# A chunked recurrent scan: growth factors in a tile of their own, operands and state updates at other levels of the inverse

## The chip, the cores and the metric

One core of a Trainium2 chip runs the whole kernel. Its engines work beside each other and meet at semaphores: TensorE (PE in the profile, with PEld for its weight loads), VectorE (DVE), ScalarE (ACT), GpSimd (POOL), and SyncE (SP), which issues most DMAs. Each engine takes its own instructions strictly in order. The metric is the device time in microseconds (us), the median of several executions.

## The reference, cut to what matters

Two layers of a diffusion backbone over 256 latent and 256 context tokens. One of the three branches of a layer is a bidirectional RWKV-7 time mixing: in each of 8 heads a 64 x 64 state is carried over the tokens, forwards and backwards.

```python
def wkv_scan(r, w, k, v, a, b, S0, reverse):
    def step(S, inp):
        rt, wt, kt, vt, at, bt = inp
        sa = jnp.einsum('bhvk,bhk->bhv', S, at)
        S = S * wt[:, :, None, :] + sa[..., None] * bt[:, :, None, :] + vt[..., None] * kt[:, :, None, :]
        return S, jnp.einsum('bhvk,bhk->bhv', S, rt)
    S_fin, ys = lax.scan(step, S0, xs, reverse=reverse)
...
y_ctx, s_ctx = rwkv_mix(pr_c, zero_state, *rw)
y_lat, _ = rwkv_mix(pr_l, s_ctx, *rw)
```

The context's final state is the start of the latent tokens' scan. In the last layer the context's outputs are not needed, only its state. Everything else (Fourier mixing, latent attention, merge, a mixture of 16 experts) is outside the change.

## The kernel before

The scan runs in chunks of 64 tokens: `STEPS` = 8 per layer, k = 0 to 3 over the context, k = 4 to 7 over the latent tokens. Each step treats both directions, d = 0 and 1, and all heads at once in tiles of 128 partitions x 256 columns (`RJ` = 4 pairs of heads x 64). Layer 0 reads an output from every step; in layer 1 `streams(l, k)` is true for k = 4 to 7 only.

What a step computes:

- `cumulate` (DVE, L1549/L1552) sums the log decays within the chunk into `L`. From it POOL subtracts (`decays_before`, L1899), and ACT makes three exponentials: `decays` into `Rq` (L1188), `decays_before` into `E3` (L1194) and `growths` (L1199), which overwrites `L`.
- `totals` (DVE, L1560) copies the last column of the decays, by which the state is scaled; `queries` (POOL, L1909) then overwrites `Rq`, so it waits for `totals`. It exists only where the step streams an output.
- `operands` (DVE, L1569 to L1571) multiplies keys with `E3` and with the growths, and signals `keys`. PE's `couple` makes the 64 x 64 coupling matrix from them, `begin` (DVE, L1577 to L1581) masks it, `grams` and `masks` (DVE, L1588 to L1592) give the others.
- The coupling matrix is inverted by doubling: `LEVELS` = 2, 4, 8, 16, 32 are n = 0 to 4 in the code and are called level zero to level four here. At each level POOL's `blocks` (L1892) picks the off-diagonal blocks, PE's `join` multiplies, ACT copies (L1237), PE's `grow` multiplies, DVE adds and transposes (L1600, L1602; the last level L1605).
- For the chunk before, k - 1, PE runs `correct` (needs the state), `solve`, `readout` and `update`; DVE's `read` adds the output (L1612) and `update` renews the state (L1620, L1621).

All PE products go through L715. The order in each engine's queue is written out by hand. PE, in step k: `couple(k)`, `correct(k-1)`, `grams(k,0)`, `solve(k-1)`, `grams(k,1)`, then five levels, each join 0, join 1, grow 0, grow 1, with the transposes of the next operands in level zero, a readout each in levels one and two, `update(k-1)` in level three and the next chunk's values in level four. PE's `correct` waits for the signal of DVE's L1621. POOL's order, which the change leaves as it is, in step k:

```python
for n in range(len(LEVELS)):
    for d in range(2):
        blocks(k, n, d)
    if more and n == 1:
        for d in range(2):
            decays_before(k + 1, d)
    if more and n >= 3:
        queries(k + 1, n - 3)
```

While a scan runs, no weights are loaded: its tiles lie where the weights go.

Of the kernel before, what the change touches and what calls it, by code (L numbers as in the profile page):

```python
# [9 lines left out]
ALU = mybir.AluOpType  # L10
ACT = mybir.ActivationFunctionType
# [23 lines left out]
DECAY = math.exp(-0.5)  # L35
# [54 lines left out]
def build(nc, xT, cT, vec, fng, rb, rw, w_ada, w_in, headw, w_ukv, lora, w_a, w_b, w_c, w_out,  # L90
# [4 lines left out]
    with ExitStack() as ctx:  # L95
# [5 lines left out]
        def sem(name):  # L101
            if name not in sems:
                sems[name] = ctx.enter_context(nc.semaphore(name))
            return sems[name]
# [70 lines left out]
        def piece(units, of=(0, 1, 2)):  # L175

            for n in of:
                if taken[n] + units * 256 <= spare[n].shape[1]:
                    taken[n] += units * 256
                    return spare[n][:, taken[n] - units * 256:taken[n]]  # L180
            raise AssertionError("no room")

        def quads(x, n=1):
            x = x.rearrange("p (x j n) -> p x j n", x=n, n=CH)
            return x if n > 1 else x[:, 0]
# [16 lines left out]
            ONCE[name] = [quads(piece(1)) for d in range(2)]  # L202
        ONCE["U"] = ONCE["RHS"]
        PF = [quads(piece(1)) for d in range(2)]
        PS = [[quads(raw[d][:, 256:512]) for d in range(2)]] * (len(LEVELS) - 1) + [PF]
        BTS = [ONCE[name] for name in ("BT0", "BT1", "BT0", "BT1", "MT")]

# [90 lines left out]
        STEPS = 2 * NCH  # L298

        def columns(k, d):  # L300

            s, c = k // NCH, k % NCH
            return slice((1 - s) * SEQ + (NCH - 1 - c if d else c) * CH, (1 - s) * SEQ + (NCH - 1 - c if d else c) * CH + CH)
# [17 lines left out]
        def nth(N, d, per=1, n=0):  # L321

            return 2 * per * N + per * d + n + 1

        def level(N, n, d):

            return 2 * (len(LEVELS) * N + n) + d + 1

        def halved(N, n, d):

# [703 lines left out]
        def _(act):  # L1034
# [31 lines left out]
            for l in range(DEPTH):  # L1066
# [116 lines left out]
                def decays(k, d):  # L1183

                    act.wait_ge(sem("cumulated"), nth(l * STEPS + k, d))
                    if k >= 2 and streams(l, k - 2):
                        act.wait_ge(sem("readout"), 2 * readouts(l, k - 2) - 1 + d)
                    act.activation(flat(TWICE["Rq"][k % 2][d]), flat(ONCE["L"][d]), ACT.Exp, scale=-DECAY)\  # L1188
                       .then_inc(sem("exps"), 1)

                def decays_before(k, d):
                    act.wait_ge(sem("before"), nth(l * STEPS + k, d))
                    x = flat(TWICE["E3"][k % 2][d])
                    act.activation(x, x, ACT.Exp, scale=-DECAY).then_inc(sem("exps"), 1)  # L1194

                def growths(k, d):
                    x = flat(ONCE["L"][d])
                    act.wait_ge(sem("exps"), nth(l * STEPS + k, d, 3, 1))
                    act.activation(x, x, ACT.Exp, scale=DECAY).then_inc(sem("exps"), 1)  # L1199

                def turns(k, d):
                    act.wait_ge(sem("turns"), carried(l, k, d))
# [2 lines left out]
                def values(k):  # L1205
                    for d in range(2):
                        act.wait_ge(sem("values"), nth(l * STEPS + k, d))
                        act.copy(flat(TWICE["Vt"][k % 2][d]), part(d, 1, 1)).then_inc(sem("values_held"), 1)
# [10 lines left out]

                log_decays(0)  # L1220
                for d in range(2):
                    decays(0, d)
                    decays_before(0, d)
                    growths(0, d)
                values(0)
                for k in range(STEPS):
                    more = k + 1 < STEPS
                    if k:
                        correct(k - 1)
                    if more:  # L1230
                        log_decays(k + 1)
                    if k:
                        solve(k - 1)
                    for n in range(len(LEVELS)):
                        for d in range(2):
                            act.wait_ge(sem("joined"), level(l * STEPS + k, n, d))
                            act.copy(under(PS[n][d], n, d), under(part(d, 3, 0).rearrange("p (j n) -> p j n", n=CH), n, d))\  # L1237
                               .then_inc(sem("joined_copied"), 1)
                            if n == 0 and more:
                                turns(k, d)  # L1240
                        if more and n in (1, 2):
                            decays(k + 1, n - 1)
                            decays_before(k + 1, n - 1)
                            growths(k + 1, n - 1)
                    if more:
                        values(k + 1)
                correct(STEPS - 1)
# [105 lines left out]
        def _(dve):  # L1353
# [22 lines left out]
            for l in range(DEPTH):  # L1376
# [164 lines left out]
                def cumulate(k, d):  # L1541

                    N, p = l * STEPS + k, k % 2
                    lw, L = TWICE["E3"][p][d], ONCE["L"][d]
                    dve.wait_ge(sem("decays"), nth(N, d))
                    if N:
                        dve.wait_ge(sem("keys"), nth(N - 1, d))
                    if d == 0:
                        dve.tensor_tensor_scan(flat(L), con_("reset", RJ * CH), flat(lw), 0.0,  # L1549
                                               ALU.mult, ALU.add).then_inc(sem("cumulated"), 1)  # L1550
                    else:
                        dve.tensor_tensor_scan(flat(L)[:, ::-1], con_("reset", RJ * CH), flat(lw)[:, ::-1], 0.0,  # L1552
                                               ALU.mult, ALU.add).then_inc(sem("cumulated"), 1)

                def totals(k, d):

                    N, p = l * STEPS + k, k % 2
                    end = CH - 1 if d == 0 else 0
                    dve.wait_ge(sem("exps"), nth(N, d, 3))
                    dve.tensor_copy(total[:, k % 3, d, :].unsqueeze(2), TWICE["Rq"][p][d][:, :, end:end + 1])\  # L1560
                       .then_inc(sem("totals"), 1)

                def operands(k, d):

                    N, p = l * STEPS + k, k % 2
                    dve.wait_ge(sem("exps"), nth(N, d, 3, 2))
                    if k:
                        dve.wait_ge(sem("turns"), carried(l, k - 1, d))
                    tt(TWICE["E3"][p][d], KK[:, :, columns(k, d)], TWICE["E3"][p][d], ALU.mult)  # L1569
                    tt(ONCE["bKk"][d], KDs[d][:, :, columns(k, d)], ONCE["L"][d], ALU.mult)  # L1570
                    tt(ONCE["bE2"][d], B[d][:, :, columns(k, d)], ONCE["L"][d], ALU.mult).then_inc(sem("keys"), 1)  # L1571

                def begin(k, d):

# [49 lines left out]
                for d in range(2):  # L1624
                    cumulate(0, d)
                for d in range(2):
                    totals(0, d)
                for d in range(2):
                    operands(0, d)
                for k in range(STEPS):  # L1630
                    more = k + 1 < STEPS
                    for d in range(2):
                        begin(k, d)
                    for d in range(2):
                        masks(k, d)
                        if more:
                            cumulate(k + 1, d)
                    for n in range(len(LEVELS)):
                        for d in range(2):
                            grow(k, n, d)  # L1640
                        if more and n in (2, 3):
                            totals(k + 1, n - 2)
                            operands(k + 1, n - 2)
                        if k and n in (1, 2):
                            read(k - 1, n - 1)
                        if k and n == 4:
                            for d in range(2):
                                update(k - 1, d)
                for d in range(2):
                    read(STEPS - 1, d)  # L1650
                over()
# [200 lines left out]
        def _(pool):  # L1852
# [15 lines left out]
            for l in range(DEPTH):  # L1868
# [25 lines left out]
                def decays_before(k, d):  # L1894

                    N = l * STEPS + k
                    pool.wait_ge(sem("cumulated"), nth(N, d))
                    x = TWICE["E3"][k % 2][d]
                    tt(x, ONCE["L"][d], x, ALU.subtract).then_inc(sem("before"), 1)  # L1899

                def queries(k, d):

                    if not streams(l, k):
                        return
                    N = l * STEPS + k
                    pool.wait_ge(sem("totals"), nth(N, d))
                    pool.wait_ge(sem("exps"), nth(N, d, 3))
                    x = TWICE["Rq"][k % 2][d]
                    tt(x, R[:, :, columns(k, d)], x, ALU.mult).then_inc(sem("queries"), 1)  # L1909

# [164 lines left out]
```

## Time and profile before

| | |
|---|---|
| median of 3 runs | 2402.03 us (2399.49 to 2406.5) |
| the profiled execution's own time | 2396.57 us |
| its span in the trace | 2394.8 us |
| PE busy | 2128.6 us, 89% of the span |
| DVE, ACT, POOL busy | 727.4, 490.0, 278.8 us |
| mean granted TensorE clock | 0.951 |
| scan of layer 0, from and to | 424.4 to 641.1 us |
| scan of layer 1 | 1651.8 to 1852.0 us |

All times in the trace are counted from the span's start. A matmul's end is modelled, so that a busy PE is a PE with work in flight. In a timeline row, the bracket at the end is how long the engine had been idle and what released it. The granted clock is 1.00 at 2.4 GHz and 0.50 at 1.2 GHz; a value between is a mean over the stretch.

### The profile page before, as it was taken

The numbers are of one execution on the slowest core, as the hardware profiler recorded it, in microseconds if no ns is written. First come the engines' busy times: TensorE is split into PE (matmuls) and PEld (weight loads), VectorE is DVE, ScalarE is ACT, GpSimd is POOL, SyncE is SP. The second block draws the span as 40 slices with busy tenths as digits, with TensorE's granted clock in tenths as the row PEclk, the third lists the DMA queues.
The fourth block names the chain that finished last, engine by engine and source line by source line (L and its number), as shares of the span: only waits on it lengthen the run. The fifth ranks groups of instructions, "written<-read, shape, count | busy, mean of one in ns | idle before, by whom it ended". The sixth has DMA issues, their size and how long they took to land. (4 is left out here: it accounts for less than half of the span.)

```text
span 2394.8 us, 53930 instructions
## 1 busy us (share of the span) xinstructions
PE 2128.6 (89%) x23930; PEld 1357.3 (57%) x23930; DVE 727.4 (30%) x1768; ACT 490.0 (20%) x1120; POOL 278.8 (12%) x463
## 2 busy tenths in 40 slices
PE   6999999899799999999999779998988899977784
PEld 2454444789644444446566464554888787744442
DVE  1023334777431011310100032445775311200001
ACT  2122322333130000301111132323332301100011
POOL 0000000444100001101111100001442000011111
PEclk8999999899999999999999989998999999989896
DMA  7149816000121312448999821210000345899993
GB/s 281 58 146 331 313 49 236 3 4 4 55 88 53 105 53 105 170 166 324 381 383 383 306 92 43 67 49 1 4 4 13 144 145 190 281 379 381 383 383 120
DMA packets 182915, 399.91 MB, mean 167 GB/s; under 512 B 6656, under 2 KB 29952, under 8 KB 182496
## 3 DMA queue, kind: packets, MB, share of 16 engines
q1 hardware_dynamic: 170528, 361.94, 42.0%
q0 software_dynamic: 8576, 23.08, 2.6%
q10 hardware_dynamic: 3648, 12.45, 1.8%
q8 instruction: 134, 2.20, 0.4%
q14 instruction: 29, 0.24, 0.0%
HBM read 365.47 MB, written 31.98 MB: 166 GB/s over the span
## 5 line engine op out<-in xcount | busy, mean ns | idle before, releaser
L481 PE MATMUL ps<-H,memory 128*128 128x512 f32 (+2 forms) x1728 | 616.7, 513 | 11.8 <-DMA memory<-in_w_in 10.0
L481 PEld LDWEIGHTS ps<-H,memory 128*128 128x128 f32 (+1 forms) x1728 | 328.8, 191 | 287.3 <-issue 251.3
L715 PE MATMUL ps<-memory 64*64 64x32 f32 (+2 forms) x10112 | 333.1, 230 | 42.9 <-DVE memory L1621 17.6
L978 PE MATMUL ps<-memory 128*32 128x256 f32 x5120 | 304.5, 400 | 60.2 <-DMA memory<-in_eu 58.6
L715 PEld LDWEIGHTS ps<-memory 64*64 64x64 f32 x10112 | 318.9, 143 | 53.9 <-DVE memory L1621 19.1
L481 PE MATMUL ps<-memory 128*128 128x512 f32 (+4 forms) x960 | 336.3, 500 | 8.3 <-issue 3.0
L978 PEld LDWEIGHTS ps<-memory 128*32 128x32 f32 x5120 | 192.0, 115 | 170.6 <-issue 89.8
L481 PEld LDWEIGHTS ps<-memory 128*128 128x128 f32 (+2 forms) x960 | 175.1, 185 | 159.1 <-issue 140.2
L1003 PE MATMUL ps<-memory 128*32 128x256 f32 x2560 | 144.8, 380 | 4.9 <-ACT memory L1324 3.8
L1892 POOL TENSOR_TENSOR memory<-memory,cons 128x256 f32<-128x256 f32 x160 | 120.3, 769 | 122.5 <-DVE memory L1577 93.0
L1956 POOL DMA_DIRECT2D expert_rows<-memory x128 | 69.3, 541 | 436.5 <-DVE memory L1825 412.6
L1003 PEld LDWEIGHTS ps<-memory 128*32 128x32 f32 x2560 | 80.0, 110 | 59.4 <-ACT memory L1324 10.1
L1260 ACT ACTIVATE memory<-ps 128x512 f32<-128x512 f32 (+1 forms) x48 | 23.5, 490 | 333.9 <-PE ps L481 333.9
L1693 DVE TENSOR_TENSOR memory<-memory,ps 128x512 f32<-128x512 f32 (+1 forms) x32 | 17.8, 555 | 214.8 <-PE ps L481 214.8
L1237 ACT COPY memory<-ps 128x128 f32<-128x128 f32 x160 | 42.9, 268 | 163.5 <-PE ps L715 163.3
L715 PE MATMUL ps<-cons,memory 64*64 64x64 f32 x1408 | 59.2, 231 | 12.5 <-issue 10.2
L1820 DVE TENSOR_TENSOR memory<-memory,ps 128x256 f32<-128x256 f32 x16 | 6.7, 421 | 183.9 <-ACT memory L1322 183.9
L715 PEld LDWEIGHTS ps<-cons,memory 64*64 64x64 f32 x1408 | 52.2, 145 | 14.8 <-issue 12.0
L1600 DVE TENSOR_TENSOR memory<-memory,ps 128x128 f32<-128x128 f32 x128 | 34.6, 270 | 81.5 <-PE ps L715 80.6
L1602 DVE STREAM_TRANSPOSE memory<-memory 128x256 f32<-128x256 f32 x128 | 57.0, 446 | 4.4
L1825 DVE COPY memory<-ps 128x256 f32<-128x256 f32 x32 | 13.6, 425 | 137.7 <-PE ps L1003 137.7
L1929 POOL TENSOR_TENSOR memory<-H 128x512 f32<-128x512 f32 (+1 forms) x2 | 2.0, 995 | 442.0 <-ACT H L1270 442.0
(251 smaller groups left out, 1808.4 us busy)
## 6 DMA issues: line engine op xcount, KB each, us to landing
memory<-in_eg SPq DMA_DIRECT2D x32, 2048.0 KB, 19.0
memory<-in_eu SPq DMA_DIRECT2D x32, 2048.0 KB, 24.9
memory<-in_ed SPq DMA_DIRECT2D x32, 2048.0 KB, 21.6
memory<-in_w_ada SPq DMA_DIRECT2D x24, 2048.0 KB, 9.9
memory<-in_w_in SPq DMA_DIRECT2D x20, 2048.0 KB, 8.4
expert_rows<-memory SPq DMA_DIRECT2D x4, 3456.0 KB, 23.6
memory<-in_w_out SPq DMA_DIRECT2D x4, 2048.0 KB, 8.0
memory<-expert_rows ACTq DMA_DIRECT2D x19, 384.0 KB, 7.0
```

Of the source, the lines that this page charges most:

```text
L481: ins = mm(ps[0:M, bank, 0:w], lhs(k), rhs(k), start=(k == 0), stop=(k == n - 1))
L715: ins = mm(out[cols, j], lhs[rows, j, :], rhs[rows, j], start=(n == 0), stop=(n == len(terms) - 1))
L978: ins = mm(out_.rearrange("p (x n) -> p x n", x=2), XGT[:, k, g * GROUP:g * GROUP + GROUP], sets[b][:, 0:2, k * 512 + c * P:k * 512 + c * ...
L1003: ins = mm(ps[cc, 6 if last else 5, at:at + 256], HIDT[:, 0, g * P + k * GROUP:g * P + k * GROUP + GROUP], sets[b][:, 2, k * D + c * 256:k ...
L1237: act.copy(under(PS[n][d], n, d), under(part(d, 3, 0).rearrange("p (j n) -> p j n", n=CH), n, d))\
L1260: act.activation(SG[:, o % 2, 0:w], ps[:, 2 * (o % 2), 0:w], ACT.Sigmoid).then_inc(sem("merge_sigmoid"), 1)
L1600: tt(x, x, under(half(d, 2, 1 - p), n, d), ALU.add).then_inc(sem("inverse"), 1)
L1602: dve.transpose(flat(TWICE["XT"][p][d]), flat(ONCE["X"][d])).then_inc(sem("inverse"), 1)
L1693: link(tt(TM[:, 0, 0:w], gate, proj, ALU.mult))
L1825: dve.tensor_copy(YG[:, b, (groups - 1) * 256:groups * 256], ps[:, 6, 0:256]).then_inc(sem("result_copied"), 1)
L1892: tt(BTS[n][d], ONCE["MT"][d], over_pairs(con_(f"lev{LEVELS[n]}")), ALU.mult).then_inc(sem("blocks"), 1)
L1956: pool.dma_start(xg[bass.ds((2 * i + b) * tr, tr), c * 256:c * 256 + 256] .rearrange("(g t) n -> t g n", t=GROUP), YG[GROUP * c:GROUP * c ...
```

## The change

The growth factors get a tile `G` and no longer overwrite `L`. ACT computes them, with the decays before each token, ahead of the decays for the readout, one level sooner. The operands move from behind levels two and three to behind levels one and two. The totals move from there to behind level three, where the state updates now follow; these stood behind level four. `grown` and `decayed` count the exponentials' signals in the new order. POOL's queue keeps its order; only the count it waits for is written anew.

```diff
+        ONCE["G"] = [quads(piece(1)) for d in range(2)]
...
+        def grown(N, d):
+
+            return 6 * N + 3 * d + 2
+
+        def decayed(N, d):
+
+            return 6 * N + 3 * d + 3
...
                 def growths(k, d):
-                    x = flat(ONCE["L"][d])
-                    act.wait_ge(sem("exps"), nth(l * STEPS + k, d, 3, 1))
-                    act.activation(x, x, ACT.Exp, scale=DECAY).then_inc(sem("exps"), 1)
+                    if l * STEPS + k:
+                        act.wait_ge(sem("keys"), nth(l * STEPS + k - 1, d))
+                    act.wait_ge(sem("cumulated"), nth(l * STEPS + k, d))
+                    act.activation(flat(ONCE["G"][d]), flat(ONCE["L"][d]), ACT.Exp, scale=DECAY).then_inc(sem("exps"), 1)
...
                 for d in range(2):
-                    decays(0, d)
                     decays_before(0, d)
                     growths(0, d)
+                    decays(0, d)
...
                         if more and n in (1, 2):
                             decays(k + 1, n - 1)
-                            decays_before(k + 1, n - 1)
-                            growths(k + 1, n - 1)
+                        if more and n < 2:
+                            decays_before(k + 1, n)
+                            growths(k + 1, n)
...
                     if N:
-                        dve.wait_ge(sem("keys"), nth(N - 1, d))
+                        dve.wait_ge(sem("exps"), decayed(N - 1, d))
...
-                    dve.wait_ge(sem("exps"), nth(N, d, 3))
+                    dve.wait_ge(sem("exps"), decayed(N, d))
...
-                    dve.wait_ge(sem("exps"), nth(N, d, 3, 2))
+                    dve.wait_ge(sem("exps"), grown(N, d))
...
-                    tt(ONCE["bKk"][d], KDs[d][:, :, columns(k, d)], ONCE["L"][d], ALU.mult)
-                    tt(ONCE["bE2"][d], B[d][:, :, columns(k, d)], ONCE["L"][d], ALU.mult).then_inc(sem("keys"), 1)
+                    tt(ONCE["bKk"][d], KDs[d][:, :, columns(k, d)], ONCE["G"][d], ALU.mult)
+                    tt(ONCE["bE2"][d], B[d][:, :, columns(k, d)], ONCE["G"][d], ALU.mult).then_inc(sem("keys"), 1)
...
                 for d in range(2):
+                    operands(0, d)
+                for d in range(2):
                     totals(0, d)
-                for d in range(2):
-                    operands(0, d)
...
                     for n in range(len(LEVELS)):
                         for d in range(2):
                             grow(k, n, d)
-                        if more and n in (2, 3):
-                            totals(k + 1, n - 2)
-                            operands(k + 1, n - 2)
+                        if more and n in (1, 2):
+                            operands(k + 1, n - 1)
                         if k and n in (1, 2):
                             read(k - 1, n - 1)
-                        if k and n == 4:
+                        if n == 3:
                             for d in range(2):
-                                update(k - 1, d)
+                                if more:
+                                    totals(k + 1, d)
+                                if k:
+                                    update(k - 1, d)
...
-                    pool.wait_ge(sem("exps"), nth(N, d, 3))
+                    pool.wait_ge(sem("exps"), decayed(N, d))
```

## Rows read from the trace of the kernel before

**Rows 1.** Windows: length; busy (x) of PE, PEld, DVE, ACT, POOL; PEclk, DMA, GB/s

```profile
424.40:641.10 216.70, 195.00 (x6016) 190.17 (x6016) 147.90 (x382) 65.94 (x207) 86.30 (x117) 0.91 0.02 4
1651.80:1852.00 200.20, 175.39 (x5504) 168.36 (x5504) 138.03 (x358) 66.01 (x207) 78.86 (x109) 0.93 0.02 4
...
479.90:507.20 27.30, 25.20 (x779) 24.50 (x770) 18.64 (x48) 8.31 (x26) 10.68 (x14) 0.94 0.02 4
507.20:533.40 26.20, 24.36 (x783) 23.59 (x774) 18.82 (x49) 8.31 (x26) 10.67 (x14) 0.93 0.02 4
533.40:557.70 24.30, 22.61 (x783) 22.22 (x774) 18.61 (x49) 8.32 (x26) 10.69 (x14) 1.00 0.02 4
...
582.00:608.10 26.10, 24.32 (x780) 23.85 (x774) 18.79 (x49) 8.31 (x26) 10.69 (x14) 0.93 0.02 4
...
631.70:638.50 6.80, 5.05 (x132) 4.73 (x134) 0.01 (x1) 1.39 (x5) 0.00 (x0) 0.50 0.02 5
...
1723.00:1745.50 22.50, 20.59 (x654) 19.56 (x644) 17.44 (x43) 8.32 (x26) 10.65 (x14) 0.92 0.02 4
```

**Rows 2.** Timeline of step 3 of layer 0, levels two to four: start, us, what, idle before

```profile
525.00 0.29 DVE L1600 TENSOR_TENSOR memory<-memory,ps 128x128 f32<-128x128 f32 x1 [1.73 <-PE ps L715]
...
526.34 0.13 DVE L1560 COPY total<-memory 128x4 f32<-128x4 f32 x1
...
526.55 0.83 POOL L1909 TENSOR_TENSOR memory<-memory 128x256 f32<-128x256 f32 x1 [4.69 <-DVE total L1560]
526.72 0.95 DVE L1570 TENSOR_TENSOR memory<-memory 128x256 f32<-128x256 f32 x1
527.34 1.77 POOL L1892 TENSOR_TENSOR memory<-memory,cons 128x256 f32<-128x256 f32 x2
...
529.01 0.29 DVE L1600 TENSOR_TENSOR memory<-memory,ps 128x128 f32<-128x128 f32 x1
...
529.41 0.57 PEld L715 LDWEIGHTS ps<-memory 64*64 64x64 f32 x16 [0.17 <-issue]
...
530.35 0.13 DVE L1560 COPY total<-memory 128x4 f32<-128x4 f32 x1
...
532.48 0.29 DVE L1605 TENSOR_TENSOR memory<-memory,ps 128x128 f32<-128x128 f32 x1 [0.20 <-PE ps L715]
...
532.91 0.69 PE L715 MATMUL ps<-memory 64*64 64x64 f32 x32 [0.49 <-DVE memory L1605]
...
534.27 0.42 DVE L1577 TENSOR_TENSOR memory<-ps,cons 128x256 f32<-128x256 f32 x1
...
534.72 0.47 PE L715 MATMUL ps<-memory 64*64 64x64 f32 x17 [1.10 <-DVE memory L1621]
```

**Rows 3.** By source line: PE's waits for L1621; POOL's L1909 idle until L1560 (us, times)

```profile
  PE ps L715: 17.6, 14
...
  DVE total L1560: 64.8, 22
```

**Rows 4.** Timeline of the end of layer 0's scan

```profile
632.07 1.98 PE L715 MATMUL ps<-memory 64*64 64x64 f32 x64 [2.28 <-DVE memory L1621]
...
641.40 0.38 SPq L364 DMA_DIRECT2D memory<-in_w_in  x1
```

**Rows 5.** Timeline of step 2 of layer 1, DVE and POOL, levels one and two

```profile
1713.01 0.45 DVE L1602 STREAM_TRANSPOSE memory<-memory 128x256 f32<-128x256 f32 x1
1714.29 0.29 DVE L1600 TENSOR_TENSOR memory<-memory,ps 128x128 f32<-128x128 f32 x1 [0.84 <-PE ps L715]
...
1713.21 1.41 POOL L1892 TENSOR_TENSOR memory<-memory,cons 128x256 f32<-128x256 f32 x2 [0.85 <-PE ps L715]
```

**Rows 6.** Timeline of the start of layer 0's scan

```profile
427.38 0.42 ACT L1199 ACTIVATE memory<-memory 128x256 f32<-128x256 f32 x1
...
428.22 0.42 DVE L1569 TENSOR_TENSOR memory<-memory 128x256 f32<-128x256 f32 x1
...
430.99 1.30 PE L715 MATMUL ps<-memory 64*64 64x64 f32 x35 [4.42 <-DVE memory L1571]
```

## Prediction

> **What bounds the kernel now.** I began with the change: every edit lies in the recurrent scan, which runs once per layer. The windows give its two runs 216.7 and 200.2 us of the 2394.8 us span, with DMA busy 0.02 of the time [rows 1]. The first load behind a scan is issued when the scan is over [rows 4]; no transfer of fixed length runs beside it that could swallow a shift. What the scan gains or loses arrives at the end in full.
>
> Inside a scan TensorE (PE) is busy 195.0 of 216.7 us; a step of layer 0 takes 24.3 to 26.2 us [rows 1]. PE's issue order thus bounds the scan, plus the places where PE waits. Where it waits longest, by the list of who waits for a line: for the state update L1621, 17.6 us in 14 waits, seven per layer [rows 3]. The timeline of step 3 shows one [rows 2]. PE runs `couple` at 532.91 (0.69 us), then needs the new state; VectorE (DVE) does the updates only behind the last inverse L1605 (532.48), and the next row is `begin` at 534.27; PE starts again at 534.72, idle 1.10.
>
> What is nearly late already matters as much. GpSimd (POOL) runs in order: in `queries(k+1, 0)` L1909 it waits for `totals`, and behind that stand both level-four `blocks` L1892. In step 3: totals 526.34, queries 526.55, blocks 527.34 to 529.11 [rows 2]. PE loads the weights of `join(k, 4, 0)`, which needs the first of them, at 529.41. So the blocks are done only 0.3 us (the first 1.2 us) before PE asks.
>
> **The change part by part.** *State updates behind level three.* Their products were issued by PE before level three's `grow`, so DVE has them. The stall goes. Each of the 14 waits returns its idle time and the modelled tail of the last matmul, some 0.23 us, less 0.03 for the next issue: 17.6 + 14 x 0.2 = 20.4 us off. Of that 2 x 2.5 is the wait behind step 7, where PE idles 2.28 us [rows 4]. The updates' 1.6 us on DVE (532.48 to 534.27, less 0.2 for the inverse) now lie between levels three and four. What hides them: PE's joins and two value transposes of level four, and the new stall below. `begin` starts at once behind `couple`, about 0.6 us sooner, as an input of the next step's masks; these waited for PE's grams, not for DVE, so nothing is taken back here.
>
> *Totals behind level three.* This is the costly part, and it is a move on DVE alone. POOL's order is untouched: `queries(k+1, 0)` still stands ahead of `blocks(k, 4, .)`. The totals go from behind level two (526.34) to behind both level-three inverses, the place of the second totals today (530.35). From DVE's first level-three inverse at D: totals at D + 1.34 (530.35 - 529.01), POOL's queries 0.21 later, its blocks 0.79 after that (527.34 - 526.55), taking 0.90 beside DVE work (1.77 for two), and 0.11 to PE's weight load (from 529.01 + 0.29 to 529.41) [rows 2]. That is D + 3.35, against D + 0.40 today: 2.95, less 0.05 because DVE reaches D a little sooner: **2.9 us** late. Everything on PE queues behind this join: next step's `values`, the second join, both `grow`. None can fill the gap. With POOL at its uncontended 0.70 per block and 0.7 for the queries it is 2.6; with step 0's extra fills 3.1. It happens where `queries(k+1)` exists: layer 0, k = 0 to 6, and layer 1, k = 3 to 6, since layer 1's context steps read nothing out: 11 steps, 11 x 2.9 = 31.9 us on (28.6 to 34.1).
>
> *Operands behind levels one and two.* Three operations of 0.42 (L1569), overlapping, cost some 1.0 us of DVE alone [rows 6], and 2.1 us beside POOL, where L1570 took 0.95 [rows 2]. Behind level one DVE idles 1.73 us in steps with readouts (until 525.00), and POOL's row before 526.55 shows it idle too: hidden [rows 2]. In layer 1's steps 0 to 2 there is neither readout nor query: DVE has 0.84 us idle before level two's inverse (1714.29) and POOL runs both blocks at 1713.21 just then [rows 5]. Operands from 1713.37 would end at 1714.37 alone, 1715.45 if they take turns with POOL: 0.1 to 1.2 us each on PE's path. Nearest row L1570: 0.95 beside POOL; I take 1.1, 3.3 us on (0 to 3.6).
> The Trainium skill, page "SBUF — State Buffer", section "SBUF: two separate sides", says GpSimd and a VectorE operation with two SBUF inputs hold the shared ports by turns, each for its whole instruction. By it, the 0.95 is a wait plus the 0.42 op, in agreement with the rows, and the collision costs its upper end.
>
> *Growth factors in their own tile.* ACT does the same exponentials, the growth one no longer in place. ACT is busy 65.9 of 216.7 us [rows 1] and nothing is issued more, so 0; without that room, each of its two moved operations would cost 0.42. The `cumulate` now waits for the last reader of L on ACT instead of DVE's keys, long past either way: 0. At a scan's start the first keys hang on this order: PE waits 4.42 us until 430.99 for L1571, and the operands at 428.22 stood behind both totals [rows 6]. With growths ahead of readout decays they start near 427.8, where the first growth L1199 ends (427.38 + 0.42), and do not meet POOL's queries: about 1.0 us in layer 0, 0.7 in layer 1, 1.7 us off (0 to 2).
>
> Sum without the clock: 31.9 + 3.3 - 20.4 - 1.7 = **+13.1 us**.
>
> **The clock.** The windows show steps at granted clock 1.00 lasting 24.3 us and steps at 0.93, which hold one stretch at 1.2 GHz, 26.1 to 26.2: 1.9 us dearer [rows 1]. Four of the middle steps hold one (from 479.9, 507.2, 582.0 and, in layer 1, 1723.0), each after a boundary with about 2.0 us of idle in two pieces. The 2.28 us stall behind step 7 was followed by 0.50 for 6.8 us [rows 1, 4]; layer 1 repeats it. Afterwards the boundary holds 0.7 us only, so the four go (-7.6), and the ends run partly at full rate (-2). But a PE stall of 3 us, longer than any that brought 1.2 GHz here, now stands in 11 steps. I take 9 of 11, at 1.6 us (less than 1.9, since the stretch covers the boundary's 0.7 too): +14.4. Net **+4.8** (between -9.6 with none and +13 with all 11 at 1.9 and no other change at the ends).
>
> Total +13.1 + 4.8 = +18 us on the profiled execution's own 2396.57 us. That execution lies 5.5 us under the median 2402.03; on the median: **2420 us**. Six microseconds of run-to-run spread make 0.3% (7.2 us) about the least that can be told from no change.
>
> **Rivals.**
> 1. *The stall is exchanged, the clock holds.* As forecast, but the new stalls bring no 1.2 GHz: +13.1 - 9.6 = +3.5, 2405.5 us, within 0.3%. For it: eight of the twelve inner boundaries with 2 us of idle kept full clock. Against: both 2.28 us stalls lost it, and the new one is longer. 0.15.
> 2. *Faster: the join does not wait for queries.* Place: POOL between L1909 and L1892 at level four. If totals were early enough, or the blocks ahead of the queries, the 31.9 drops out: -18.8 - 9.6 = -28, 2374 us. It decides below (20.4 + 1.7 - 3.3) / 11 = 1.7 us per queried step, clock aside. For it: the waits on L1621 are the biggest in the scan, and in step 3 PE got level four's first blocks 1.2 us before it asked. Against: the loop order of POOL in the listing, and the waits 64.8 us in 22 of L1909 on totals [rows 3]: POOL already sits there each step until DVE gets to them. 0.07.
> 3. *The dear end.* POOL chain at 3.1, clock down in all 11 steps at 1.9, collisions in full: 34.1 + 3.6 - 20.4 + 21 - 7.6 - 1 = +30, 2432 us. 0.18.
> 4. The forecast, 2420 us (2411 to 2429): 0.60.
>
> **From these to the numbers.** Slower by over 0.3%: cases 3 and 4 and the upper edge of 1: 0.80. Within 0.3%: the rest of 1 and what the unequal gains of steps may add, 0.13. Faster: 0.07. The range leaves out case 2 and some of the dear end: 2404 to 2433.
>
> **What would show it.** After the change: (a) no PE wait on L1621; `correct` follows `couple` at once. (b) Eleven PE waits on POOL's blocks, near 3 us each, before the fourth join; steps in layer 1 with k = 0 to 2 without them. (c) L1909's start moves behind level three, and L1892 starts 0.7 to 0.9 us behind it. (d) In layer 1's first three steps level two's inverse starts about 1 us later behind level one. (e) Layer 0's steps last 24.3 + 2.9 - 1.3 = 25.9 us at full clock, 27.5 with a stretch at 1.2 GHz; the scans total near 228 and 206 us. (f) Outside the scans nothing moves. The prediction is wrong if (b) is missing or its waits are below 1.7 us, and its size is wrong if the granted clock in those steps stays 1.00.

## The result and the profile after

The changed kernel takes 2445.41 us (median of 4 runs, 2442.42 to 2447.9) beside 2402.75 for the one before: 1.0158, 95% interval [1.0125, 1.0191]. Run again beside a new group of runs (e9) it gave 1.0125 [1.0088, 1.0162] (2440.04 against 2410.28). So it is slower by some 30 to 43 us; the forecast was 2420 us, slower by 18, and its range ended at 2433 us.

The profiled execution of the changed kernel takes 2447.54 us, its span 2445.8. Its windows, in the columns of [rows 1]: both scans, steps 3, 4 and 6 of layer 0, and step 1 of layer 1.

```profile
426.40:664.40 238.00, 208.46 (x6016) 204.36 (x6016) 142.25 (x383) 64.42 (x207) 84.22 (x117) 0.84 0.01 4
1675.40:1900.00 224.60, 196.77 (x5504) 190.99 (x5504) 137.40 (x359) 64.38 (x207) 78.30 (x109) 0.81 0.01 3
518.30:547.60 29.30, 26.05 (x782) 25.72 (x779) 18.27 (x48) 8.17 (x26) 10.44 (x14) 0.85 0.02 3
547.60:576.90 29.30, 26.05 (x778) 25.72 (x775) 18.29 (x48) 8.16 (x26) 10.42 (x14) 0.85 0.01 4
605.40:634.40 29.00, 25.43 (x782) 24.89 (x776) 18.07 (x48) 8.16 (x26) 10.43 (x14) 0.88 0.01 4
1706.70:1731.10 24.40, 22.83 (x652) 22.10 (x645) 16.79 (x42) 8.09 (x26) 8.83 (x12) 0.80 0.02 4
```

The scans grew from 216.7 and 200.2 us [rows 1] to 238.0 and 224.6. The granted clock fell from 0.91 and 0.93 to 0.84 and 0.81. Since it is either 1.00 or 0.50, the time at 1.2 GHz is the scan's length times twice what the mean lacks to 1.00: 39 and 28 us before, 76 and 85 us after.

The list by source line says who waits for POOL's blocks (first line, L1892 before) and how long POOL's queries idle for the totals (second).

```profile
  PE ps L724: 30.3, 11
...
  DVE total L1571: 96.6, 12
```

Eleven PE waits, 2.75 us each. Before, PE had no such wait. The second line was 64.8 us in 22 waits [rows 3]. The timeline of step 3 of layer 0 shows the chain behind one of them; L1611 is level three's first inverse, L1571 the totals, L1922 the queries, L1905 the blocks, L1632 the state update, L1588 `begin`.

```profile
538.38 0.29 DVE L1611 TENSOR_TENSOR memory<-memory,ps 128x128 f32<-128x128 f32 x1 [1.20 <-PE ps L724]
...
539.72 0.13 DVE L1571 COPY total<-memory 128x4 f32<-128x4 f32 x1
...
539.93 0.72 POOL L1922 TENSOR_TENSOR memory<-memory 128x256 f32<-128x256 f32 x1 [8.61 <-DVE total L1571]
540.21 0.73 DVE L1632 TENSOR_TENSOR memory<-memory,total 128x256 f32<-128x256 f32 x1
540.61 1.59 POOL L1905 TENSOR_TENSOR memory<-memory,cons 128x256 f32<-128x256 f32 x2
...
541.57 0.66 PE L724 MATMUL ps<-memory 64*64 64x32 f32 x16 [2.76 <-POOL memory L1905]
...
546.77 3.04 PE L724 MATMUL ps<-memory 64*64 64x64 f32 x100 [0.49 <-DVE memory L1616]
547.93 0.42 DVE L1588 TENSOR_TENSOR memory<-ps,cons 128x256 f32<-128x256 f32 x1 [1.30 <-PE ps L724]
```

Read it as the forecast's sum: totals 1.34 us behind the inverse, queries 0.21 later, blocks 0.68 later, PE 0.96 after that; 3.19 us instead of 3.35. At 546.77 `couple`, `correct` and what follows are one unbroken row of 100 matmuls: the wait for the update [rows 2] is gone. What stands behind the wait is the surprise (windows of the same kernel: PE's wait in step 3, what follows it, and what follows the wait in step 4):

```profile
536.00:541.50 5.50, 2.81 (x98) 2.70 (x93) 4.20 (x13) 0.27 (x1) 1.57 (x3) 1.00 0.02 3
542.40:552.60 10.20, 9.71 (x234) 9.61 (x231) 4.79 (x13) 2.30 (x8) 3.67 (x5) 0.50 0.01 3
573.10:579.90 6.80, 6.31 (x166) 6.21 (x164) 3.14 (x8) 1.86 (x7) 0.99 (x2) 0.50 0.02 5
```

Within a microsecond of PE's resuming (541.57) the clock falls to 1.2 GHz and stays there for 10.2 us, through the rest of level four, `couple`, `correct` and the grams. Ten of the eleven waits have such a stretch, which begins within 1.6 us of PE's resuming: two of 3.4 us, two of 6.8 and six of 10.2, 8.2 us in the mean. At the eleventh, in step 0 of layer 0, the clock was low already. Before, the four such stretches behind a step's boundary lasted 3.4 us each.

### The profile page after: what moved, and what is told of

Read it like the earlier page. It is cut to its first block and busy times, and to the rows that moved or that the text cites. A ratio compares the mean times of both kernels' runs of the same rounds, so it can differ in the third digit from the quotient of the medians.

```text
span 2445.8 us, 53960 instructions
## 1 busy us (share of the span) xinstructions
PE 2169.7 (89%) x23930; PEld 1400.9 (57%) x23930; DVE 720.7 (29%) x1768; ACT 486.8 (20%) x1120; POOL 276.3 (11%) x463
## 5 line engine op out<-in xcount | busy, mean ns | idle before, releaser
L724 PE MATMUL ps<-memory 64*64 64x32 f32 (+2 forms) x10112 | 359.6, 244 | 53.6 <-POOL memory L1905 30.3
L724 PEld LDWEIGHTS ps<-memory 64*64 64x64 f32 x10112 | 348.2, 157 | 62.4 <-POOL memory L1905 32.6
L1905 POOL TENSOR_TENSOR memory<-memory,cons 128x256 f32<-128x256 f32 x160 | 118.8, 759 | 146.0 <-DVE memory L1588 117.1
L1969 POOL DMA_DIRECT2D expert_rows<-memory x128 | 69.3, 541 | 437.9 <-DVE memory L1838 416.9
L1012 PEld LDWEIGHTS ps<-memory 128*32 128x32 f32 x2560 | 80.0, 110 | 59.4 <-ACT memory L1335 10.1
L724 PE MATMUL ps<-cons,memory 64*64 64x64 f32 x1408 | 65.5, 252 | 12.3 <-issue 10.2
L724 PEld LDWEIGHTS ps<-cons,memory 64*64 64x64 f32 x1408 | 58.2, 164 | 14.7 <-issue 11.8
L1611 DVE TENSOR_TENSOR memory<-memory,ps 128x128 f32<-128x128 f32 x128 | 34.5, 269 | 86.2 <-PE ps L724 85.9
L511 PE MATMUL ps<-memory 128*32 128x512 f32 x384 | 47.7, 617 | 4.8 <-DMA memory<-in_w_ada 4.4
## 6 DMA issues: line engine op xcount, KB each, us to landing
memory<-in_eu SPq DMA_DIRECT2D x32, 2048.0 KB, 24.8
expert_rows<-memory SPq DMA_DIRECT2D x4, 3456.0 KB, 23.6
```

The source lines that it names most:

```text
L511: ins = mm(ps[32 * g:32 * g + 32, bank, :], CP[:, k, at:at + 32], slot(n, "ADA")[:, k * 512:k * 512 + 512], start=(n == first and k < 4), ...
L724: ins = mm(out[cols, j], lhs[rows, j, :], rhs[rows, j], start=(n == 0), stop=(n == len(terms) - 1))
L1012: ins = mm(ps[cc, 6 if last else 5, at:at + 256], HIDT[:, 0, g * P + k * GROUP:g * P + k * GROUP + GROUP], sets[b][:, 2, k * D + c * 256:k ...
L1611: tt(x, x, under(half(d, 2, 1 - p), n, d), ALU.add).then_inc(sem("inverse"), 1)
L1905: tt(BTS[n][d], ONCE["MT"][d], over_pairs(con_(f"lev{LEVELS[n]}")), ALU.mult).then_inc(sem("blocks"), 1)
L1969: pool.dma_start(xg[bass.ds((2 * i + b) * tr, tr), c * 256:c * 256 + 256] .rearrange("(g t) n -> t g n", t=GROUP), YG[GROUP * c:GROUP * c ...
```

## The experiments

All ratios are to the kernel before on the same chip; they are not exactly the quotients of the medians (for e7 that would be 1.0260, for e11 0.9980), and the text goes by the ratios. "Changed" is the kernel after the change.

| run | from | ratio | 95% interval | median us |
|---|---|---|---|---|
| e1_queries_last | changed | 0.9968 | [0.9947, 0.9988] | 2398.9 |
| e2_filler | changed | 1.0036 | [1.0015, 1.0057] | 2414.09 |
| e3_updates_alone | before | 0.9970 | [0.9949, 0.9991] | 2398.53 |
| e4_totals_back | changed | 0.9939 | [0.9918, 0.9960] | 2394.35 |
| e5_apart | e4 | 0.9922 | [0.9885, 0.9958] | 2389.7 |
| e6_operands_apart | changed | 1.0140 | [1.0106, 1.0174] | 2435.92 |
| e7_totals_alone | before | 1.0282 | [1.0242, 1.0321] | 2467.93 |
| e8_warm_start | e5 | 0.9936 | [0.9914, 0.9959] | 2390.22 |
| e9_changed_again | changed | 1.0125 | [1.0088, 1.0162] | 2440.04 |
| e10_filler_small | changed | 1.0095 | [1.0069, 1.0121] | 2433.2 |
| e11_boundary_filler | before | 1.0000 | [0.9976, 1.0024] | 2405.39 |

The medians of the kernel before in the three groups were 2406.49 (e1 to e4), 2405.32 (e5 to e8) and 2410.28 us (e9 to e11).

**e1: POOL's order alone.** Totals, updates and operands stay at their new places; only the queue of POOL is turned.

```diff
-                        if more and n >= 3:
-                            queries(k + 1, n - 3)
+                        if more and n == 4:
+                            for d in range(2):
+                                queries(k + 1, d)
```

> The changed kernel, but POOL issues both queries behind both level-four blocks. Theory A (the added time is the POOL chain totals, queries, blocks, and the 1.2 GHz stretches that its stalls bring): the eleven PE waits on POOL's blocks vanish, the low clock in the queried steps with them, 2402 - 20 (update waits) - 2 (start) + 3 (collisions) - 8 (clock) = 2375 us, +-6. Theory B (totals and updates between levels three and four, or operands beside POOL, cost the time, whatever POOL's order): still above 2420 us.

The eleven waits on the blocks are gone and the loss with them: 0.9968. Theory B is out: with late totals and early updates in place the kernel is no slower than before. But 2375 us was not reached; where the missing time lies is read under e4.

**e4: totals back.** The other way to free POOL.

```diff
+                        if more and n in (2, 3):
+                            totals(k + 1, n - 2)
                         if more and n in (1, 2):
                             operands(k + 1, n - 1)
...
-                        if n == 3:
+                        if k and n == 3:
                             for d in range(2):
-                                if more:
-                                    totals(k + 1, d)
-                                if k:
-                                    update(k - 1, d)
+                                update(k - 1, d)
```

> The changed kernel, with the totals back behind levels two and three (ahead of the operands), updates behind level three. Theory A (the late totals make the stall): no PE waits on POOL's blocks, like the kernel with the queries last, 2375 us +-6. Theory B (operands and updates at their new places cost the time): above 2420 us.

0.9939: two independent ways of freeing the blocks both undo the whole loss. The miss against 2375 us has two parts. The first can be read in layer 0's steps at full clock. Windows of steps 4 and 5 of this kernel:

```profile
532.50:556.10 23.60, 22.76 (x779) 22.22 (x771) 18.31 (x48) 8.11 (x26) 10.61 (x14) 1.00 0.02 5
556.10:579.80 23.70, 22.93 (x787) 22.42 (x777) 18.30 (x48) 8.11 (x26) 10.61 (x14) 1.00 0.02 4
```

They last 23.6 and 23.7 us where those of before last 24.3 [rows 1]: a wait in which PE was idle for 1.1 us (the forecast counted 1.3 with the tail of the last matmul) vanished, and the step is only 0.6 to 0.7 us shorter. Of the idle times of matmuls (PE) and weight loads (PEld) in two such steps, three of the kernel before (us, times, longest), then three of e4:

```profile
PEld ps L715 <- DVE memory L1621: 2.4, 2, 1.2
PE ps L715 <- DVE memory L1621: 2.2, 2, 1.1
PEld ps L715 <- issue: 1.5, 4, 0.6
```

```profile
PEld ps L724 <- issue: 2.2, 6, 0.6
PE ps L724 <- DVE memory L1616: 1.0, 2, 0.5
PE ps L724 <- issue: 0.4, 2, 0.2
```

The update's line is gone, and idle time that nothing in the profile releases ("issue") has grown over two steps from 1.5 to 2.2 us on the weight loads and from nothing to 0.4 us on the matmuls. Set beside each other matmul by matmul, step 4 of e4 is 0.85 us ahead of that of before once `correct` is through, and loses 0.2 us of it again in level zero, where PE shows no idle time. Why is open.

The second part is layer 1. From step 0's `begin` to step 7's, layer 0 went from 176.9 us to 165.8 in the profiled executions, but layer 1 from 160.5 to 167.0, and its time at 1.2 GHz in that stretch from 13.5 to 40.7 us. Windows of steps 1 and 2 of layer 1, first of the kernel before, then of e4:

```profile
1680.40:1700.90 20.50, 19.24 (x652) 18.30 (x643) 15.19 (x40) 8.31 (x26) 8.63 (x12) 1.00 0.02 4
1700.90:1723.00 22.10, 19.17 (x651) 18.33 (x648) 16.02 (x44) 8.31 (x26) 8.66 (x12) 1.00 0.02 4
```

```profile
1677.80:1702.10 24.30, 22.58 (x649) 21.80 (x644) 16.84 (x42) 8.11 (x26) 8.87 (x12) 0.80 0.02 4
1702.10:1726.10 24.00, 21.89 (x656) 21.09 (x648) 16.82 (x42) 8.11 (x26) 8.81 (x12) 0.86 0.01 4
```

In these steps nothing waits for POOL's blocks; what does slow them is asked under e5 and e6.

**e7: the late totals alone**, in the kernel before.

```diff
                         if more and n in (2, 3):
-                            totals(k + 1, n - 2)
                             operands(k + 1, n - 2)
+                        if more and n == 3:
+                            for d in range(2):
+                                totals(k + 1, d)
```

> The kernel before, with only the totals moved behind level three; operands and updates stay. Theory A (one late copy makes the whole loss): eleven PE waits on POOL's blocks near 2.9 us, 31.9 us, and 1.2 GHz stretches after each, 20 us or more, while the waits for the updates stay: 2450 to 2465 us. Theory B (the loss needs the updates between levels three and four as well): below 2430 us.

1.0282, 2467.93 us: theory A, a little above its range. By source line, PE waits for the blocks:

```profile
  PE ps L715: 39.6, 11
```

3.6 us each instead of 2.75. Here the second operands, too, stand ahead of the totals on DVE, some 1.0 us of work. A step (window of step 3 of layer 0):

```profile
517.90:549.10 31.20, 26.37 (x782) 25.90 (x775) 16.93 (x48) 8.38 (x26) 10.06 (x14) 0.85 0.01 3
```

Two copies of 128 x 4 elements, 0.13 us of work each, moved behind level three and its operands, cost 63 us by the medians.

**e2 and e10: work in place of idle.** In the changed kernel, PE is given products that nobody reads, ahead of level four's first join: 40 in e2, 16 in e10 (each product stands as two matmul records in a trace). The edit of e2; e10 has `range(2)` in place of `range(5)`:

```diff
                     for n in range(len(LEVELS)):
+                        if n == 4 and more and streams(l, k + 1):
+                            for _ in range(5):
+                                heads(None, (part(0, 3, 1), (V[:, :, columns(k, 0)], eye, 0, 0)))
                         join(k, n, 0)
```

> The changed kernel, with 40 products of 64x64 that nothing reads issued on PE into a free PSUM half just ahead of the fourth join of each step that has queries, about 2.3 us of PE work inside a wait of 2.9. Theory A1 (some 30 of the 43 us are the clock: the wait itself is worth 13 net, the 1.2 GHz that follows it the rest): the wait stays but PE is busy in it, the granted clock in layer 0's steps returns to 0.95 or more, and the time falls to 2410 to 2420 us. Theory A2 (the clock is not set by this wait, or costs little): 2440 us or more, since nothing else is shortened.

> The changed kernel with 16 products that nothing reads (0.9 us at full clock) ahead of the fourth join of each queried step, instead of the 40 of the second run. The open question is whether the clock's cost follows the idle left over. Theory A1 (what is left idle in the stretch decides): about 2 us of each wait stay, as much as the boundaries of the kernel before had; part of the 31 us that the full filler gave comes back, 10 to 25 us: 2420 to 2435 us. Theory A3 (any PE work inside the wait keeps the clock): 2412 to 2418 us, like the full filler. Theory A4 (only a full wait of work helps): 2440 us or more.

e2: 1.0036, that is 21 to 29 us less than the changed kernel (from its two ratios), with more work and the same chain. Windows of steps 3 and 4 of layer 0:

```profile
505.30:531.90 26.60, 24.89 (x863) 24.48 (x853) 18.07 (x48) 8.11 (x26) 10.43 (x14) 1.00 0.02 4
531.90:558.50 26.60, 25.05 (x864) 24.61 (x856) 18.08 (x48) 8.10 (x26) 10.45 (x14) 1.00 0.02 5
```

26.6 us at clock 1.00, against 29.3 at 0.85: the clock is worth 2.7 us a step, and theory A1 holds. What is left, 26.6 - 24.3 = 2.3 us more than a full-clock step of before, is the new wait less what the vanished update wait gave; against e4's 23.6 and 23.7 us it is 2.9 to 3.0. The chain on DVE and POOL is untouched.

With 16 products PE still idles 1.8 us in a wait, in the mean. The runs spread from 2416.54 to 2441.8 us (1.0095), and the profiled execution, the fastest of the eight, holds both kinds of step (steps 2 and 3 of layer 0):

```profile
482.80:509.20 26.40, 23.74 (x813) 23.20 (x803) 18.09 (x48) 8.12 (x26) 10.45 (x14) 1.00 0.02 4
509.20:537.10 27.90, 25.25 (x816) 24.78 (x811) 18.07 (x48) 8.17 (x26) 10.44 (x14) 0.94 0.02 4
```

So with part of the wait filled the clock holds in one step and not in the next, and the median lies in theory A1's range. It is not established by the whole times: e10's interval overlaps that of e9, the changed kernel in the same group (1.0088 to 1.0162).

**e3: the updates alone**, in the kernel before, behind the operands and totals of level three.

```diff
-                        if k and n == 4:
+                        if k and n == 3:
                             for d in range(2):
                                 update(k - 1, d)
```

> The kernel before, with only the state updates moved from behind level four to behind level three (behind the second totals and operands). Both theories: the 14 PE waits on the updates vanish, 20.4 us, and with them the four 1.2 GHz stretches at the boundaries, up to 8 us: 2374 to 2384 us. If instead the updates delay the last inverse, so that the wait only moves: 2395 us or more.

0.9970: some gain, far from 2374 to 2384. The wait moved. By source line, PE now waits for the last inverse L1605 (6.8 us in 14 waits before), and the timeline shows it queued behind the updates, which are queued behind the operands:

```profile
  PE ps L715: 19.4, 14
```

```profile
557.32 0.42 DVE L1621 TENSOR_TENSOR memory<-memory,total 128x256 f32<-128x256 f32 x1
557.66 0.48 DVE L1605 TENSOR_TENSOR memory<-memory,ps 128x128 f32<-128x128 f32 x2
559.00 0.42 DVE L1577 TENSOR_TENSOR memory<-ps,cons 128x256 f32<-128x256 f32 x1 [0.86 <-PE ps L715]
```

Both inverses run back to back, so both had been ready. A full-clock step of e3 takes 24.8 us, no less than the 24.3 of before, where e4's takes 23.6 to 23.7: the updates pay only with the operands out of their way. By the whole times alone this would be argued, for the intervals of e3 and e4 overlap by a hair (0.9949 and 0.9960).

**e5 and e6: the collision.** In the three steps of layer 1 without queries both operands go behind level two. e5 is e4 with this, e6 the changed kernel with this.

```diff
-                        if more and n in (1, 2):
+                        if more and streams(l, k + 1) and n in (1, 2):
                             operands(k + 1, n - 1)
+                        if more and not streams(l, k + 1) and n == 2:
+                            for d in range(2):
+                                operands(k + 1, d)
```

> The changed kernel with the totals back behind levels two and three, and, in the three steps of layer 1 that have no queries to feed, both operands behind level two, where POOL is idle. Theory A (in those steps the operands behind level one take turns with POOL's blocks, 1.1 us each on PE's path, and the clock falls with it): they go from 24.0 to 24.7 us back to 21 to 22.5, layer 1's scan from 202 to some 194 us, the kernel 6 to 9 us below the one with the totals back: 2385 to 2389 us, beside 2394 for that one. Theory B (layer 1's steps are long for another reason, a clock that is low since the scan's start): 2392 us or more.

> The changed kernel with nothing mended but these three steps' operands (both behind level two). Theory A: the late totals and their eleven waits stay; only the collision goes, 3.3 us and the 1.2 GHz stretches that come with it in three steps, some 9 us in all: 2434 to 2440 us. Theory B (the collision costs nothing of its own): 2443 us or more.

First the collision itself, in the timeline of step 1 of layer 1 of the changed kernel, DVE and then POOL:

```profile
1717.73 0.45 DVE L1613 STREAM_TRANSPOSE memory<-memory 128x256 f32<-128x256 f32 x1
1718.10 0.84 DVE L1580 TENSOR_TENSOR memory<-memory 128x256 f32<-128x256 f32 x1
1718.86 0.94 DVE L1581 TENSOR_TENSOR memory<-memory 128x256 f32<-128x256 f32 x1
1719.73 0.41 DVE L1582 TENSOR_TENSOR memory<-memory 128x256 f32<-128x256 f32 x1
1720.07 0.28 DVE L1611 TENSOR_TENSOR memory<-memory,ps 128x128 f32<-128x128 f32 x1
```

```profile
1717.93 1.59 POOL L1905 TENSOR_TENSOR memory<-memory,cons 128x256 f32<-128x256 f32 x2 [0.74 <-PE ps L724]
```

Operands take 1.97 us instead of 1.0, and the inverse of level two starts 2.34 us behind the transpose (1717.73) instead of 1.28 [rows 5]: 1.1 us late, as forecast. PE itself idles 1.8 us in three waits for that inverse L1611, one in each of steps 0 to 2. Steps 1 and 2 of layer 1 in e6, against 24.4 and 24.1 us in the changed kernel, and step 2 in e5:

```profile
1698.20:1718.90 20.70, 19.16 (x652) 18.28 (x643) 15.95 (x42) 8.11 (x26) 8.62 (x12) 1.00 0.02 4
1718.90:1740.30 21.40, 19.01 (x645) 18.18 (x648) 16.14 (x42) 8.10 (x26) 8.64 (x12) 1.00 0.02 4
```

```profile
1695.40:1718.90 23.50, 21.86 (x652) 21.14 (x643) 16.08 (x42) 8.11 (x26) 8.62 (x12) 0.85 0.02 4
```

About three microseconds a step in e6, of which at most 1.1 is the collision; the rest goes with the clock, 0.80 in the changed kernel's step 1 and 1.00 here. But e5 has the same edit, and its step 2 still runs at 0.85, its steps 3 and 4 hold 6.8 us at 1.2 GHz each, with no PE wait above 0.8 us near them. So the collision is not the only thing that brings the low clock to layer 1; what else does is open. The medians, 2389.7 and 2435.92 us, lie just above theory A's range in e5 and within it in e6. In whole times e6's interval overlaps that of the changed kernel (1.0140 to 1.0125 and 1.0158), and e5's that of e4, so the gain of e5 over e4 (4 us by the ratios) is not established. e5 has the lowest ratio of all, 0.9922: 0.4 to 1.2% faster than before, with single runs from 2374.84 to 2396.0 us.

**e8: filling the scan's first wait.** e5 with 32 unread products behind the first values.

```diff
                 for d in both:
                     values(0, d)
+                for _ in range(4):
+                    heads(None, (part(0, 3, 1), (V[:, :, columns(0, 0)], eye, 0, 0)))
```

> The kernel of the first run of this group (totals back, operands apart), with 32 products that nothing reads on PE at each scan's start, inside its wait of 3.4 us for the first keys. Theory A1 (idle time alone brings the low clock): less of the first steps runs at 1.2 GHz, 2 to 5 us less than without. Theory A2 (the first steps are short of work anyway): the same within 0.1%.

Within the error of e5 (0.9936 and 0.9922). No gain shows, but e5's interval is as wide as 0.4% to either side, so the 2 to 5 us of theory A1 are not ruled out.

**e11: the boundary's clock, in the kernel before.**

```diff
                     couple(k)
+                    if k >= 2:
+                        for _ in range(2):
+                            heads(None, (part(0, 3, 1), (V[:, :, columns(k - 1, 0)], eye, 0, 0)))
                     if k:
                         correct(k - 1)
```

> The kernel before, with 16 products that nothing reads in each step's wait for the state update (0.9 of 1.3 us). It measures the sum's term for the four 1.2 GHz stretches at the boundaries. If they come from this idle time and cost 1.9 us each: 5 to 8 us less than before, 2397 us or so, and no such stretch in the steps from 1 on. If they come from elsewhere: no change, or 1 to 3 us more.

No change, 1.0000. Windows of steps 3 and 4 of layer 0 and PE's waits in steps 4 and 5:

```profile
505.60:530.90 25.30, 23.91 (x813) 23.32 (x809) 18.80 (x49) 8.32 (x26) 10.72 (x14) 1.00 0.02 4
530.90:556.60 25.70, 24.16 (x814) 23.38 (x808) 18.69 (x49) 8.42 (x26) 10.70 (x14) 1.00 0.02 4
```

```profile
PEld ps L715 <- issue: 3.6, 7, 1.1
PE ps L715 <- issue: 1.7, 3, 0.8
```

The clock is at 1.00 in step 3, where it was 0.93 [rows 1], but a full-clock step now takes 25.3 to 25.7 us instead of 24.3. Products of 0.9 us put into a wait of 1.1 us of idle cost 1.0 to 1.4 us, and over two steps the "issue" idle is up from 1.5 to 3.6 us on the weight loads and from nothing to 1.7 us on the matmuls. In layer 0 no step from 2 to 6 holds a 1.2 GHz stretch any more, as the first case has it; in layer 1 steps 2 and 3 hold 6.8 us each, where before step 3 alone held 3.4. So the run neither prices the stretches nor shows them gone; it shows that filling a wait of this PE queue was not free.

**e9: the changed kernel again.**

> The changed kernel itself, beside the two fillers on the same chip. Both theories: 1.3 to 1.9% above the kernel before.

1.0125, at the lower edge of what was expected, and the measure for e10.

## Why the prediction was wrong

The sign held, and so did the mechanism of the stall; the size did not. Two terms of the sum were mis-sized: the clock, by some 20 us, and the state updates, by some 9. The sum should be set against the two scans together, 462.6 us after and 416.9 before [rows 1]: 45.7 us in the profiled executions, of 51 in all; the rest lies outside the scans and within the spread of single executions.

- **Totals behind level three, +31.9.** Right. Eleven waits, in the steps named, 30.3 us of PE idle; e1, e4 and e7 show from both sides that the copy's place ahead of POOL's queries is the cause. The chain measured 3.19 us for 3.35.
- **Operands, +3.3.** Right in mechanism: the inverse is 1.1 us late in the step shown. PE's own idle is 1.8 us over the three steps, so 3.3 is the upper end. Its consequence for the clock there was not foreseen.
- **Start, -1.7.** Right. PE's first coupling starts 431.88 - 426.4 = 5.5 us into layer 0's scan, against 430.99 - 424.4 = 6.6 [rows 6]; in layer 1 it is 5.7 against 6.3.
- **State updates, -20.4.** Too large. The inner waits vanished, but a full-clock step is shorter by only 0.6 to 0.7 of their 1.3 us (e4). The one behind step 7 shrank from 2.28 us [rows 4] only to 0.74 (0.59 in layer 1), by some 1.6: there the updates stand ahead of the last inverse, and the second still ends after PE has nothing else left. With 12 x 0.65 + 2 x 1.6 this term is about -11.

```profile
656.18 1.16 PE L724 MATMUL ps<-memory 64*64 64x64 f32 x64 [0.74 <-DVE memory L1632]
```

- **The clock, +4.8.** This is the step that failed most. "I take 9 of 11, at 1.6 us": a stretch came at ten of the eleven waits, but 8.2 us long in the mean, where I had taken the 3.4 us and the price of those before. My own rows pointed the other way: the wait of 2.28 us behind step 7, the nearest to the new one, was followed by 6.8 us at 0.50 [rows 1, 4], while the steps' boundaries, with some 0.49 + 1.10 = 1.6 us of PE idle [rows 2], gave 3.4 us in only four cases of twelve. e2 prices the new stretches without a model: a step 2.7 us shorter, the kernel 21 to 29 us. And the term had nothing for layer 1's steps 0 to 2, which have no such wait: they grew by 8.5 us in all, with the time at 1.2 GHz up from 10.1 to 34.2 us.

The terms then add up: 30.3 + 3.3 - 11 - 1.7 = 21 without the clock (19 with the operands at 1.8), and 45.7 - 21 = 25 for the clock (26), where the forecast had 4.8. That is a remainder, not a measurement. e2's 21 to 29 us are the eleven waits' share alone, since in e2 layer 1's steps 0 to 2 last 24.1 to 24.7 us as in the changed kernel; how much the old stretches gave back, and what those three steps add, the runs do not tell apart. Why one stretch is 3.4 us long and the next 10.2 is not shown. Why a removed wait gives back only half is open too: e4 and e11 show the amount, no run shows the cause.

Rival 1, that the clock holds, was wrong in the direction that mattered; rival 3, the dear end at 2432 us, had the right idea with too small a price. Rival 2 is the kernel that e1 builds, and it lands at 2398.9 us, not 2374: the update waits gave back half, and in layer 1 its time at 1.2 GHz rose, from step 0's `begin` to step 7's, from 13.5 to 48.1 us.

## What to carry to other kernels

Before an operation is moved on one engine, look at which other engine's in-order queue waits for it, and at what stands behind that wait: here a 0.13 us copy held two block selections that PE needed. A PE stall is priced as its length plus what the time at 1.2 GHz behind it costs, and here the second equalled the first (2.7 and 2.75 us); take that price from the row whose stall is nearest in length, and test it by giving PE unread work in the stall. And where PE issues small matmuls back to back, count half of a removed wait until a run shows more.

## What the runs showed of the hardware

- PE idles of 2.75 us in steps otherwise full of matmuls were followed by 3.4 to 10.2 us at granted clock 0.50, ten times in eleven; one of 2.28 us by 6.8 us; some 1.6 us in two pieces at a step's boundary by 3.4 us, four times in twelve. With 40 unread products in the 2.75 us the clock stayed at 1.00 in layer 0's steps 1 to 6.
- Removing a wait with 1.1 us of PE idle shortened a step by 0.6 to 0.7 us, in a stretch of 64x64 and 64x32 matmuls some 30 ns apart (780 records in 23.6 us); 0.2 us a step came back as "issue" idle of the matmuls.
- L1632, a DVE operation on two SBUF operands, took 0.73 us beside POOL's queries instead of 0.42.
